# Attention scores as row tiles: two heads and two query blocks in four banks, attended two blocks at once

## What is computed

```python
def attend(q_nope, q_rope, k_nope, k_rope, v):
    scale = (QK_NOPE + QK_ROPE) ** -0.5
    s = jnp.einsum('bqhd,bkhd->bhqk', q_nope, k_nope) + jnp.einsum('bqhr,bkr->bhqk', q_rope, k_rope)
    p = jax.nn.softmax(s.astype(jnp.float32) * scale, axis=-1).astype(v.dtype)
    return jnp.einsum('bhqk,bkhd->bqhd', p, v)
```

## Time and profile before

| | |
|---|---|
| median of three runs | 1222.69 us |
| profiled execution | 1222.99 us, its span 1221.2 us |
| PE, weight loads, DVE, ACT, POOL busy | 98%, 82%, 71%, 43%, 16% |
| mean granted clock of TensorE | 0.999 of full speed |
| HBM traffic | 154 GB/s over the span |

### The profile page before, as it was taken

One profiled execution on the slowest core, in us unless ns is written; L12 is line 12 of the kernel. 1 busy time (PEld: TensorE's weight loads), 2 busy tenths in 40 slices (PEclk: granted clock), 3 DMA queues, 4 the chain that ended last, 5 costly groups with the idle time before them and its releaser, 6 DMA issues.

```text
span 1221.2 us, 17807 instructions
## 1 busy us (share of the span) xinstructions
PE 1199.4 (98%) x6834; PEld 997.7 (82%) x6834; DVE 866.6 (71%) x1286; ACT 530.0 (43%) x891; POOL 191.9 (16%) x158
## 2 busy tenths in 40 slices
PE   7999999999999999999999999999999999999997
PEld 5777777788888898888888888889879999888886
DVE  4675766586887487678765666699887877766666
ACT  4342565522534352222222223465664555655554
POOL 0106993000001200000000000302980002000000
PEclk9999999999999999999999999999999999999999
DMA  9956322134464436557664665335434674666662
GB/s 296 315 153 206 84 54 69 36 86 132 110 178 131 156 105 191 152 163 217 187 193 153 209 192 157 101 90 149 122 114 113 168 212 138 201 196 190 181 198 87
DMA packets 265252, 188.88 MB, mean 155 GB/s; under 512 B 16035, under 2 KB 250833, under 8 KB 265169
## 3 DMA queue, kind: packets, MB, share of 16 engines
q1 hardware_dynamic: 264832, 187.60, 52.7%
q10 hardware_dynamic: 337, 0.15, 0.0%
HBM read 186.67 MB, written 1.05 MB: 154 GB/s over the span
## 4 chain that ended last, share of the span: by engine, by line
PE 89%; DVE 3%; ACT 3%; SPq 2%; issue 2%; DMA 1%; ACTq 0%; DVEq 0%
PE bank L2081 18%; PE bank L2083 17%; PE bank L2082 17%; PE bank L2122 5%; PE bank L2120 3%; PE scores L2570 3%; PE bank L2550 2%; PE bank L2552 2%; PE bank L2551 2%; PE probsT L2579 2%; PE attended L2593 1%; SPq L494 1%; ACT Whi L402 1%; DVE Wlo L413 1%; PE bank L2649 1%
## 5 line engine op out<-in xcount | busy, mean ns | idle before, releaser
L413 DVE TENSOR_TENSOR Wlo<-Wraw,Whi 128x1024 fp32r<-128x1024 f32 (+3 forms) x294 | 323.3, 1108 | 104.2 <-ACT Whi L402 103.1
L402 ACT ACTIVATE Whi<-Wraw 128x1024 fp32r<-128x1024 f32 (+1 forms) x296 | 270.4, 928 | 125.6 <-PE bank L2083 72.0
L2081 PE MATMUL bank<-Hhi,Whi 128*128 128x512 f32 (+1 forms) x786 | 285.6, 363 | 1.7 <-DVE Wlo L413 1.4
L2082 PE MATMUL bank<-Hlo,Whi 128*128 128x512 f32 (+1 forms) x786 | 281.6, 358 | 0.0
L2083 PE MATMUL bank<-Hhi,Wlo 128*128 128x512 f32 (+1 forms) x786 | 281.5, 358 | 0.0
L2081 PEld LDWEIGHTS bank<-Hhi,Whi 128*128 128x128 f32 x786 | 148.4, 189 | 30.6 <-issue 6.6
L2082 PEld LDWEIGHTS bank<-Hlo,Whi 128*128 128x128 f32 x786 | 148.5, 189 | 22.2 <-issue 1.0
L2083 PEld LDWEIGHTS bank<-Hhi,Wlo 128*128 128x128 f32 x786 | 148.5, 189 | 22.0
L2081 PE MATMUL bank<-Uhi,Whi 128*128 128x512 f32 (+1 forms) x350 | 128.3, 367 | 0.2 <-issue 0.2
L2083 PE MATMUL bank<-Uhi,Wlo 128*128 128x512 f32 (+1 forms) x350 | 126.5, 362 | 0.0
L2082 PE MATMUL bank<-Ulo,Whi 128*128 128x512 f32 (+1 forms) x350 | 126.5, 361 | 0.0
(11 more groups left out here) (309 smaller groups left out, 1977.6 us busy)
## 6 DMA issues: line engine op xcount, KB each, us to landing
Wraw<-in_w_ff SPq DMA_DIRECT2D x126, 512.0 KB, 3.9
Wraw<-in_w_in SPq DMA_DIRECT2D x78, 512.0 KB, 4.0
ATT<-in_w_mod SPq DMA_DIRECT2D x58, 512.0 KB, 4.5
Wraw<-in_w_o SPq DMA_DIRECT2D x16, 512.0 KB, 4.1
ACC<-in_w_mod SPq DMA_DIRECT2D x14, 512.0 KB, 4.4
Wraw<-in_w_mla_o SPq DMA_DIRECT2D x8, 512.0 KB, 3.5
ATT<-in_w_mod SPq DMA_DIRECT2D x12, 256.0 KB, 8.4
Wraw<-in_w_kv_b SPq DMA_DIRECT2D x12, 256.0 KB, 4.1
```

The costliest lines, as they stand in the source:

```text
L402: last = act.activation(hi, raw, ACT.Copy)
L413: last = eng.tensor_tensor(lo, raw, hi.bitcast(F32), ALU.subtract)
L2081: pe.matmul(dst, sh, mh, start=j == 0, stop=False)
L2082: pe.matmul(dst, sh, ml, start=False, stop=False)
```

## The change

Scores are computed as row tiles: the plain part of a block is two matmuls over 64 rows each, one for each head, on the two halves of the array's rows; the rotary part of two blocks is four matmuls over 32 rows each, accumulated on top. The operands get a layout for it: QN and KN hold both heads' plain parts one below the other, QR two blocks' and two heads' rotary queries in four strips, KR4 the rotary key four times. Scores have four banks, the two old ones and banks 2 and 3 of the ring, which has two during attention. Two blocks are attended at once, with 256 columns moving. The orders of PE and ACT are written anew, gate parts are cut differently, and PE waits for both rotary query additions at the start of a pair.

```diff
-    b = self.ring % 4
+    b = self.ring % self.width
...
-        Qb = ATT[:, 0:2 * T].rearrange("p (h n) -> p h n", h=2)
-        Kb = ATT[:, 2 * T:4 * T].rearrange("p (h n) -> p h n", h=2)
-        PTs = ATT[:, 4 * T:6 * T].rearrange("p (h n) -> p h n", h=2)
+        QN, QR, KN, KR4 = (ATT[:, i * T:(i + 1) * T] for i in range(4))
...
+        PTs = [w.rearrange("p (k n) -> p k n", k=4) for w in (ATT[:, 4 * T:6 * T], GATE_ROW)]
+        SCORES = [S[0], S[1], banks[2], banks[3]]
...   ScalarE
-                    for h in range(2):
-                        last = act.activation(Kb[0:NOPE, h, :], banks[t.bank][h * NOPE:(h + 1) * NOPE, :], ACT.Copy)
-                    last.then_inc(drained[t.bank], 1)
+                    act.activation(KN, banks[t.bank][:, :], ACT.Copy).then_inc(drained[t.bank], 1)
...
+                    exp(0, 0)
+                    exp(0, 1)
                     look(next(looks))
                     gate_a = at.tile()
+                    if l == 0:
+                        for h in range(2):
+                            copy(0, h)
+                            exp(1, h)
+                        gate_out(gate_a, p * 2)
+                        look(next(looks))
+                        for h in range(2):
+                            copy(1, h)
+                        for h in range(2):
+                            exp(2, h)
+                        if not last:
+                            next_keys()
+                        for h in range(2):
+                            copy(2, h)
+                            exp(3, h)
+                        if not last:
+                            queries_out(following[1])
+                        for h in range(2):
+                            copy(3, h)
+                    else:
+                        copy(0, 0)
+                        gate_out(gate_a, p * 2)
+                        exp(1, 0)
+                        copy(0, 1)
+                        exp(1, 1)
+                        look(next(looks))
+                        if not last:
+                            next_keys()
+                        copy(1, 0)
+                        if not last:
+                            queries_out(following[1])
+                        copy(1, 1)
...   VectorE
-                for h in range(2):
-                    mark(dve.tensor_copy(Kb[64:96, h, :], KR))
+                for i in range(4):
+                    mark(dve.tensor_copy(KR4[i * ROPE:(i + 1) * ROPE, :], KR))
...
-                        dve.tensor_tensor(Qb[NOPE:NOPE + ROPE, h, 0:TQ], Z[i:i + ROPE, 0, 0:TQ], Z[i:i + ROPE, 1, 0:TQ],
-                                          add).then_inc(q_ready, 1)
+                        dve.tensor_tensor(QR[2 * ROPE * e:2 * ROPE * (e + 1), 0:NS[l] * P].rearrange("p (g n) -> p g n", n=P),
+                                          half_turned[:, :, e, :], turned_half[:, :, e, :], add).then_inc(q_ready, 1)
...   TensorE
+                def nope_scores(d):
 
                     col, k0, kt = duos[d]
+                    for h in range(2):
+                        rows = slice(h * NOPE, (h + 1) * NOPE)
+                        pe.matmul(SCORES[2 * (d % 2) + h][:, 0:kt * P], QN[rows, col:col + P],
+                                  KN[rows, k0 * P:(k0 + kt) * P], start=True, stop=False)
+
+                def rope_scores(g):
+
+                    _, k0, kt = duos[2 * g]
+                    for i in range(4):
+                        rows = slice(i * ROPE, (i + 1) * ROPE)
+                        pe.matmul(SCORES[i][:, 0:kt * P], QR[rows, g * P:(g + 1) * P],
+                                  KR4[rows, k0 * P:(k0 + kt) * P], start=False, stop=True).then_inc(qk_done, 1)
...
-                            last = pe.matmul(PV[h * VH:(h + 1) * VH, col:col + P],
+                            last = pe.matmul(PV[h * VH:(h + 1) * VH, col:col + SEQ],
                                              V[:, k0 + k, (2 * p + h) * VH:(2 * p + h + 1) * VH],
-                                             PTs[:, h, k * P:(k + 1) * P], start=k == 0, stop=k == kt - 1)
+                                             PTs[h][:, k, :], start=k == 0, stop=k == kt - 1)
...
+                    at.heads.n += 2
+                    pe.wait_ge(q_ready, at.heads.n)
+                    pe.wait_ge(drained[keys.bank], keys.drained)
+                    pe.wait_ge(drained[nopes.bank], nopes.drained)
+                    nope_scores(0)
...
+                    nope_scores(1)
+                    rope_scores(0)
                     if l == 0:
+                        gate_a = gate_parts(4, 6, 8)
...
+                        next(gate_a)
+                        turn(0, 0)
+                        next(gate_a)
+                        turn(0, 1)
+                        next(gate_a)
+                        turn(1, 0)
+                        nope_scores(2)
+                        turn(1, 1)
+                        nope_scores(3)
+                        rope_scores(1)
+                        if more:
+                            keys = keys_tile()
+                        else:
+                            next(gate_b)
+                        attend(p, 1)
+                        turn(2, 0)
...
                     else:
                         gate_a = gate_parts(8)
+                        if not more:
+                            gate_b = gate_parts(2, 4, 6, 8)
+                        else:
+                            gate_b = gate_parts(4, 8) if fours else gate_parts(2, 6, 8)
+                        next(gate_a)
+                        turn(0, 0)
+                        if more:
+                            keys = keys_tile()
+                        else:
                             next(gate_b)
+                        turn(0, 1)
+                        if more:
+                            slot = chunk()
+                            nopes = query_tile(slot, 0)
                         else:
+                            next(gate_b)
+                        turn(1, 0)
+                        if fours:
+                            query_tile(slot, 1)
+                        else:
+                            next(gate_b)
+                        turn(1, 1)
+                        next(gate_b)
+                        attend(p, 1)
```

More of the change, by code:

```diff
@@ L140, in __init__ @@
         self.uses = [Tally() for _ in range(4)]
-        self.ring = 0
+        self.ring, self.width = 0, 4
         self.z = 0
@@ L994, in copies @@
-                    def copies(d, heads=range(2)):
-                        kt = duos[d][2]
[L997 to L1003, removed]
+                        act.wait_ge(max_done, at.unit.n + (2 * d + h + 1))
@@ L1004, in pair, with next_keys @@
+                    def next_keys():
+                        following.extend(at.tile() for _ in range(3 if queries_kind(p + 1) == "fours" else 2))
+                        act.wait_ge(qk_done, at.unit.n + 2 * len(duos))
+                        keys_out(following[0])
+                    following = []
+                    exp(0, 0)
+                    exp(0, 1)
                     look(next(looks))
                     gate_a = at.tile()
[L1006 to L1017, removed]
-                    copies(len(duos) - 1, [1] if not last and len(following) == 2 else range(2))
+                    if l == 0:
[30 more added lines that the diff above has]
+                        copy(1, 1)
@@ L1027, in pair @@
                     at.unit.n += 2 * len(duos)
-                    at.duo.n += len(duos)
+                    at.duo.n += len(duos) // 2
+                at.width = 2
                 for p in range(PAIRS):
                     pair(p)
+                at.width = 4
                 nxt = ahead(["plain"] * 4 + branch_kinds(l) * 4, ["plain"] * AHEAD)
@@ L2582, in attend @@
                 def attend(p, d):
-                    col, k0, kt = duos[d]
-                    if d == 0 and p:
+                    col, k0, kt = duos[d - 1]
+                    if d == 1 and p:
                         pe.wait_ge(op_lo, at.operand.n)
-                    if d == 0 and p == 0:
-                        for t in vt:
-                            pe.wait_ge(drained[t.bank], t.drained)
                     pe.wait_ge(turned_copied, at.unit.n + 2 * d + 2)
@@ L2606, in _ @@
                     else:
                         gate_a = gate_parts(8)
-                        gate_b = gate_parts(2, 4, 8) if more else gate_parts(4, 6, 8)
-                    next(gate_a)
-                    for d in range(len(duos) - 1):
-                        turn(d, 0)
-                        for h in range(2):
-                            scores(d + 1, h)
-                        turn(d, 1)
-                        if d == 0 and l == 0:
-                            next(gate_a)
-                        elif not more:
+                        if not more:
+                            gate_b = gate_parts(2, 4, 6, 8)
+                        else:
```

(24 more changed lines are left out.)

74 lines of the change are left out of this document (34 added, 40 removed).

## The result

The changed kernel takes 1240.32 us (median of four runs, 1236.61 to 1242.83), the kernel before beside it 1222.90: ratio 1.0137 [1.0125, 1.0149], 17.4 us slower. Forecast were 1231.7 us and a range of 1222 to 1242. The sign was right and the measured time lies in the range, the size was half of it: 9.0 us forecast, 17.4 measured. Of these, 7.7 us come by the mechanism that was forecast; the rest comes from two things that the sum left out, as the experiments show.

What follows compares the result with a forecast made beforehand. PE was taken to bound both attention stretches while the softmax chain stays hidden. Exposed chain less work saved gave +3.8 + 4.6 + 0.6 = +9.0 us on 1222.99: 1232.0, median 1231.7; own range 1227 to 1237, stated 1222 to 1242.

Steps and rivals of the forecast that it cites:

- rival 1: Layer 0 and 1 rotary bursts take twice as long, row tiles sharing less than column tiles: +8.5, 1240 us; 12%.
- +3.8 for layer 0: Layer 0 attention: each pair saves 0.53 us of PE work, loses 1.76 to waits; +1.2 for three pairs, +0.3 last.
- +0.6 for the entry: Entry to layer 1: four rotary key copies on VectorE and PE waiting for both query additions start it 0.6 us later.
- +4.6 for layer 1: Layer 1 attention: new waits less 0.71 us of work saved a pair: +0.86, +1.15, +0.86, and +1.70 in the last.
- 4.9 us of work saved: PE work in attention falls by 2.1 us in layer 0 and 2.8 in layer 1, over 8 pairs.
- Turn(1,1) of layer 0: PE's transposes of block 1, second head: held by ScalarE's copy until R + 9.23, a wait of 1.26 us.
- R: End of the rotary burst on PE, where the scores of all four banks become complete together.
- The bank in layer 1: The tile after block 1's first transposes waits 1.46 us for ScalarE to drain the keys from the ring's second bank.
- Turn(1,0) of layer 0: PE's transposes of block 1, first head: held by VectorE's scaling until R + 6.84, a wait of 0.5 us.
- Rival 2: Changes of tile shape on PE, 44 of 0.13 us in the sum, are free: some 1226 us; 12%.
- 0 to +2 in all, none taken: GpSimd stretching VectorE's low part of the weights, then on the path: 0 to +2 us, costed at nothing.
- Rival 3: In both layers the softmax chain stays covered, so the 4.9 us of work saved show: 1217 us; 12%.

Runs made afterwards that it cites:

- experiment 7: The kernel before the change with 27 of GpSimd's 28 convolution taps left out in each layer: 1222.62 us, ratio 0.9997.
- experiment 8: The changed kernel with 27 of GpSimd's 28 convolution taps left out in each layer: 1230.33 us, ratio 1.0058.
- experiment 1: The changed kernel with idle matmuls put into PE's new waits, writing a bank that nothing reads yet: 1234.61 us, ratio 1.0093.
- Experiment 9: Experiment 5's kernel with PE's wait for rotary queries moved to just ahead of the rotary burst, VectorE's key copies behind the rotary products: 1223.12 us.
- experiment 5: The changed kernel with ScalarE's block 1 copies (layer 1: also the keys' copy) and VectorE's block 1 maxima ahead of the weight split: 1223.23 us, ratio 1.0003.
- experiment 6: Experiment 5's ScalarE and VectorE orders with row tiling undone (96-row scores, one matmul for plain and rotary part): 1226.17 us, ratio 1.0028.
- experiment 4: The changed kernel with only row tiling undone (96-row scores, one matmul for plain and rotary part), its new order kept: 1232.56 us, ratio 1.0085.
- experiment 3: The changed kernel with only VectorE's order altered, block 1's row maxima ahead of the weight split and layer 1's tap: 1227.97 us, ratio 1.0042.

## Why the prediction was right in sign and short in size

**How right it was.** The sign was forecast, and 1240.32 us lies in the stated 1222 to 1242. But the sum's own range was 1227 to 1237, and the measured time is outside it. The upper end of 1242 stood there for rival 1, dear rotary bursts, and these did not come; two other things filled that room. That is luck.

**Where 17.4 us are.** 7.7 us are order and tiles (experiments 7 and 8). The other 9.7 are GpSimd and clock; 5.7 of them are the clock (experiment 1), so 4.0 are left to GpSimd's stretch itself. Each of these holds to 2 or 3 us, by the spread of the change's runs. The line between the last two is not sharp: the falls in layer 0 stand behind waits that GpSimd has lengthened, and go with it.

**The sum** had +3.8 for layer 0, +0.6 for the entry and +4.6 for layer 1. Without GpSimd the traces show +3.6 (0.4 of it ahead of the first scores), +0.1 and +3.9. They come so near because two errors offset each other. The sum counted some 17 us of waits and had 4.9 us of work saved. Without GpSimd PE is idle for 4.6 and 6.3 us in the two stretches, where the kernel before has some 1, and is yet only 7.2 us slower there, so that the work saved is 2.7 us. The waits of the kernel before were read too large as well: 0.9 us in layer 0's last pair and 0.3 to 0.7 in each of layer 1's, where the windows of before have PE idle for 0.4 in the one and for 0.1 to 0.3 in the others. And 1.2 for three pairs and 0.3 make 3.9 in layer 0, not 3.8.

**The waits** were right where ScalarE's queue sets them. Turn(1,1) of layer 0: put at R + 9.23, measured in the third pair, whose rotary burst is over at 206.59, R + 9.11, a wait of 1.16 for 1.26. The bank in layer 1: 1.30 for 1.46. Where VectorE's queue sets them they were put too long. Turn(1,0) of layer 0: R + 6.66 for 6.84, so that its wait of 0.5 is only 0.14 (213.25 where 213.11 was free). Layer 1: 0.72 in the change's first pair looks like the forecast 0.79, but a tap of 0.96 us beside GpSimd is in it; with GpSimd idle it is 0.22 (experiment 8). The last pair of layer 1 was put at 2.9 us of waits and has 1.01 and 0.59.

**The entry** to layer 1 cost 1.0 us for 0.6, and not at the place foretold. PE does not wait for the query additions at the first scores; it waits 0.60 us one tile earlier, for a bank that VectorE's rotary products read (873.10, L1683). Experiment 9 takes this wait away.

**PE's work** was wrong for the short bursts. The group of 512 keys takes 2.99 us to the start of the next tile, 2.95 forecast; the tile's first matmul then takes 0.11 more than its 0.23, so 3.10 in all:

```profile
140.31 1.13 PE L2590 MATMUL scores<-ATT 64*128 64x512 f32 x4
141.28 1.02 PE L2590 MATMUL bank<-ATT 64*128 64x512 f32 x4
142.23 0.70 PE L2598 MATMUL scores<-ATT 32*128 32x512 f32 x2
...
142.77 0.59 PE L2598 MATMUL scores<-ATT 32*128 32x512 f32 x2
...
143.30 0.50 PE L2577 MATMUL bank<-Hhi,Whi 128*128 128x512 f32 x1
```

(the rows of the other two banks, which start 0.01 to 0.02 later, are left out). The four row tiles do run at once, so rival 1 falls. But the two passes of the rotary burst start 0.54 and 0.53 apart, not 0.43, and with 256 columns (experiment 5: 153.88 to 154.53) it is 0.65 for two where 0.43 is streaming. So some 0.10 us stands over in each pass of four tiles, at 512 columns as at 256. I had put the surplus down to three changes of shape; for 512 keys the two accounts give the same. For the 256-key blocks they don't: with the two turns (0.44 each) taken off, 3.27 us leave 2.39, where 1.28 of columns, five changes and the loads made 2.14. The pairs of layer 0 show what that does: with the chain covered (experiment 5) they take 26.2, 28.1 and 26.1 us from score to score, before 26.3, 28.3 and 26.2, so that the 0.53 us of work saved in each are 0.2 at most. Four row tiles are thus worth 4 x 0.43 / 0.53 = 3.2 times at 512 columns and 4 x 0.215 / 0.325 = 2.6 at 256. The Trainium skill's 3.07 (TensorE: Matmul & The Clock Gate, Measured speedup vs the span model) is nearer to the first than the "nearly four" that I took from the column tiles. Rival 2, some 1226 us with changes at no price, falls as a forecast: a group takes 2.99 and not 2.56. What a change costs by itself these rows don't separate from the surplus of the passes; the pass across the change to 128 rows (0.53) is no longer than the one within the shape.

**GpSimd's stretch** is a term that failed: "0 to +2 in all, none taken". The row for it was there: one low part at 1.96 us. I priced that one instruction; the scalings too are open to it, in all the pairs beside which GpSimd works, and the earlier trace rows shows it busy for 51.91 of 104.80 us. The trace of before has such a scaling as well, of 1.33 us for 0.49 (at 144.55). It is hidden before (experiment 7: 0.4 us, no difference) and on the path after.

**The clock** was taken at full speed throughout, because the earlier trace rows shows 1.00. Those rows hold for a PE with 1 us of idle time in the stretch. Nothing in them tells what PE's idle time of 2 us in one piece does, and the prediction made such pieces without pricing it.

**Costed at nothing** and seen otherwise: the joined copies. They save 0.59 of ScalarE in each pair of layer 1, and where the copies end a wait for the bank that counts (experiment 6). The prediction had it in its 0.60, so the sum does not suffer.

**Rival 3**, the chain stays covered, was the right question at a wrong price. Covered by hand (experiment 5) the kernel is level with before and not 5.7 us faster, because the work saved is less (short bursts) and layer 1 and its entry keep 3.2 us of waits.

**What stays open.** The surplus of 0.10 us in each pass: no run separates weight loads, changes of shape and the issue of eight instructions. What in PE's idle time brings the half clock: single waits of 2.0 to 2.2 us have it behind them, and so do two that add up to 2.0 in the third pair of layer 1. But two that add up to 2.0 and 2.1 in the pairs ahead of it don't, nor do single ones of 1.95 and 1.87 in experiment 4, nor four of 1.1, a pair's length apart (experiment 3). No run varies it alone. Which of the two engines is stretched when VectorE and GpSimd meet is open too; the traces show either.

## To carry to other kernels

- A regrouping that saves columns on PE also takes away cover. Before costing the columns, lay each engine's queue in order from the moment when the scores are complete to the instruction that PE wants, and count what stands in front of it; here a weight split of 0.95 us on ScalarE and a low part of 1.14 on VectorE stood there for later work, and putting the chain ahead of them was worth 17.1 us, the falls of the clock and GpSimd's stretch with it.
- When an instruction moves from behind cover onto the path, its price reaches up to the longest that the trace shows for it, and belongs in the range: look which neighbour works beside it in each pair. Here even that was not the top: 1.96 us in the trace of before, 2.31 in the change's.
- Here small tiles paid some 0.10 us more in each pass of four. With 512 columns row tiles won 0.3 us a group, with 256 they lost 0.7.

## What was not expected of the hardware

- Idle times of PE of 2.0 to 2.2 us were followed by stretches of 3.4, 6.8 and 3.4 us at a granted clock of 0.50, the lower level; others, of 1.9 to 2.1 us, were not. Work of no use in those waits made the kernel 5.7 us faster.
- Beside GpSimd the low part of a weight took 2.31 us for 1.23, and the scaling of 512 columns 1.42 for 0.49, nearly three times, in its longest case (others 0.7 to 0.8); the maxima out of PSUM kept their 1.27. Elsewhere the low part kept its 1.21 and GpSimd's own instruction took 2.34 us for 1.3.
- Four 32-row tiles of float32 ran at once, in four banks, at 0.53 us a pass of 512 columns for 0.43.
